# Single chunks beside the attention pairs of the last two layers, in place of groups

## The reference, cut to what matters

```python
h = rms_norm(x, norm_mix_pre)
proj = h @ w_in                      # dq, dk, dv, mq, mk, mv, c_q, c_kv, k_pe, g
oa = diff_attention(dq1, dq2, dk1, dk2, dv, lam, bias)   # 4 heads, softmax1 - lam * softmax2
oa = rms_norm(oa, diff_subln) * (1 - lam_init)
ob = moba_attention(mq, mk, mv, bias)                    # 4 heads, one block here: causal
oc = causal_attention(q_of(c_q), k_of(c_kv, k_pe), v_of(c_kv))   # "mla", 8 heads
br = [oa @ w_branch[0], ob @ w_branch[1], oc @ w_branch[2]]
mixed = sum(sigmoid(g[i]) * br[i]) @ w_out
x = x + rms_norm(mixed, norm_mix_post)
h = rms_norm(x, norm_mlp_pre)
x = x + rms_norm(square(relu(h @ w_up)) @ w_down, norm_mlp_post)
```

## Time and profile before

| | us |
|---|---|
| median of three runs | 3230.31 |
| lowest, highest | 3227.36, 3231.82 |
| the profiled run | 3227.58 |
| its span, from the first to the last instruction | 3225.8 |
| busy of the span: PE, DVE, ACT | 3094.3, 1801.9, 1152.2 |
| mean granted clock of PE | 0.974 |

### The profile page before, as it was taken

The page is one execution under the profiler, slowest core; times in us unless marked ns, Lnnn a source line. Parts: engine busy times, 40 slices in busy tenths (PEclk is TensorE's granted clock), DMA queues, the critical chain, the costliest instruction groups (busy, mean ns, idle before and its releaser), DMA issues. The chain is left out here.

```text
span 3225.8 us, 45812 instructions
## 1 busy us (share of the span) xinstructions
PE 3094.3 (96%) x18901; PEld 2696.4 (84%) x18901; DVE 1801.9 (56%) x3335; ACT 1152.2 (36%) x1943; POOL 62.2 (2%) x106
## 2 busy tenths in 40 slices
PE   7999999999989999999999898999999999999998
PEld 4788887888867888878888787999788999888998
DVE  1767665435447896643333444556656665656565
ACT  2322223223323222232222444444444444354443
POOL 1000000000000000000000100000001000001000
PEclk9899999999999999999999899999999999999999
DMA  8346442122124566532423323566335454435452
GB/s 272 109 133 183 138 156 89 42 83 92 59 66 135 167 213 183 180 101 72 117 76 109 91 81 84 166 179 196 98 100 183 147 190 133 131 92 167 135 183 92
DMA packets 501207, 421.28 MB, mean 131 GB/s; under 512 B 9946, under 2 KB 497674, under 8 KB 501000
## 3 DMA queue, kind: packets, MB, share of 16 engines
q1 hardware_dynamic: 497976, 412.33, 41.8%
q0 software_dynamic: 3024, 6.03, 0.8%
HBM read 417.20 MB, written 1.12 MB: 130 GB/s over the span
## 5 line engine op out<-in xcount | busy, mean ns | idle before, releaser
L1271 DVE TENSOR_TENSOR w_low<-raw,w_high 128x1024 fp32r<-128x1024 f32 (+2 forms) x720 | 761.4, 1099 | 367.0 <-ACT w_high L857 365.6
L857 ACT ACTIVATE w_high<-raw 128x1024 fp32r<-128x1024 f32 (+2 forms) x720 | 648.3, 950 | 689.9 <-PE gemm L1881 410.3
L1881 PE MATMUL gemm<-xh,w_high 128*128 128x512 f32 (+1 forms) x1792 | 676.6, 378 | 21.0 <-DVE xl L1307 21.0
L1881 PE MATMUL gemm<-xl,w_high 128*128 128x512 f32 (+1 forms) x1792 | 666.7, 372 | 0.0
L1881 PE MATMUL gemm<-xh,w_low 128*128 128x512 f32 (+1 forms) x1792 | 666.2, 372 | 0.0
L1881 PEld LDWEIGHTS gemm<-xh,w_high 128*128 128x128 f32 x1792 | 341.4, 191 | 92.1 <-issue 17.3
L1881 PEld LDWEIGHTS gemm<-xh,w_low 128*128 128x128 f32 x1792 | 341.7, 191 | 63.1
L1881 PEld LDWEIGHTS gemm<-xl,w_high 128*128 128x128 f32 x1792 | 342.2, 191 | 60.3 <-issue 0.7
L1881 PE MATMUL gemm<-yh,w_high 128*128 128x256 f32 x1216 | 351.3, 289 | 16.3 <-DVE yl L1332 7.1
L1881 PE MATMUL gemm<-yl,w_high 128*128 128x256 f32 x1216 | 346.3, 285 | 0.0
L1881 PE MATMUL gemm<-yh,w_low 128*128 128x256 f32 x1216 | 345.7, 284 | 0.0
(11 more groups left out here) (326 smaller groups left out, 4224.6 us busy)
## 6 DMA issues: line engine op xcount, KB each, us to landing
raw<-in_ffn_w_in SPq DMA_DIRECT2D x176, 512.0 KB, 5.2
raw<-in_w_mod SPq DMA_DIRECT2D x72, 1024.0 KB, 7.0
raw<-in_w_in SPq DMA_DIRECT2D x50, 1024.0 KB, 5.3
raw<-in_w_up SPq DMA_DIRECT2D x32, 1024.0 KB, 5.5
raw<-in_w_down SPq DMA_DIRECT2D x32, 1024.0 KB, 5.1
raw<-in_ffn_w_out SPq DMA_DIRECT2D x32, 768.0 KB, 4.7
raw<-in_ret_w_in SPq DMA_DIRECT2D x24, 1024.0 KB, 5.2
raw<-in_ffn_w_out SPq DMA_DIRECT2D x32, 640.0 KB, 4.3
```

The source lines that it names most:

```text
L857: act.activation(wh[i % SPL][:, a:b], raw[slot_of["w", i]][:, a:b], ACT.Copy).then_inc(w_high, 1)
L1271: dve.tensor_tensor(wl[slot][:, a:b], raw[slot][:, a:b], wh[i % SPL][:, a:b].bitcast(F32), ALU.subtract).then_inc(w_low, 1)
L1881: ins = pe.matmul(out, l_, r_, start=first and j == 0, stop=last and j == 2)
```

## The change

`alongside` gets a rule for each kind of attention: with x the step, diff has (x + 1) // 2 items done, moba min(4, 1 + (x + 1) // 2), mla x + (x + 1) // 2; nat keeps its own. All three engines pass by_chunk=True to the projections beside diff and mla, so that an item is a chunk: 8 beside diff, 24 beside mla. gate0 is stepped by chunks too; where one `next` stood, two stand. Its last four chunks run beside moba through `alongside`, on ACT and DVE with lag 1. On PE a small generator puts the wait for the scaled diff outputs (sub_t) behind moba's first scores, as before.

```diff
--- before.py
+++ after.py
@@ -669,11 +669,11 @@
 
 
             a = atts[name]
-            na, nb = 2 * len(a.pairs), 24 if a.nat else 4 if a.kind == "dif" else 12
             done = 0
-            for x in range(na + 1):
+            for x in range(2 * len(a.pairs) + 1):
                 next(steps)
-                upto = min(nb, x - x // 13) if a.nat else 1 + x * (nb - 2) // na
+                upto = {"nat": min(24, x - x // 13), "dif": (x + 1) // 2, "mob": min(4, 1 + (x + 1) // 2),
+                        "mla": x + (x + 1) // 2}[a.kind]
                 while done < upto - lag:
                     next(rest)
                     done += 1
@@ -1186,23 +1186,24 @@
                 run(gemm(f"diff_v{l}1"))
                 run(gemm(f"mla_ukv{l}"))
                 run(gemm(f"moba_q{l}"))
-                alongside(f"diff{l}", attention(f"diff{l}"), both(*(gemm(o) for o in with_diff(l))), 1)
-
-                gate = gemm(f"gate0{l}")
+                alongside(f"diff{l}", attention(f"diff{l}"), both(*(gemm(o, by_chunk=True) for o in with_diff(l))), 1)
+
+                gate = gemm(f"gate0{l}", by_chunk=True)
                 for hd in range(DH):
                     act.wait_ge(o_high, atts[f"diff{l}"].p0 + 2 * hd + 2)
                     act.activation(yt[:, hd, :], oraw[:, hd, :], ACT.Square).then_inc(sub_sq, 1)
+                next(gate)
                 next(gate)
                 act.wait_ge(sub_ms, l + 1)
                 act.activation(root8[:, :], aux[3][:, 0:8], ACT.Sqrt, bias=eps[:, 0:1],
                                scale=1.0 / P).then_inc(sub_root, 1)
                 next(gate)
+                next(gate)
                 for hd in range(DH):
                     act.wait_ge(sub_t, DH * l + hd + 1)
                     act.activation(ah[:, hd, :], oraw[:, hd, :], ACT.Copy, scale=1.0 - LAM_INIT[l]).then_inc(sub_high, 1)
-                run(attention(f"moba{l}"))
-                run(gate)
-                alongside(f"mla{l}", attention(f"mla{l}"), both(*(gemm(o) for o in with_mla(l))), 1)
+                alongside(f"moba{l}", attention(f"moba{l}"), gate, 1)
+                alongside(f"mla{l}", attention(f"mla{l}"), both(*(gemm(o, by_chunk=True) for o in with_mla(l))), 1)
                 for q in range(4):
                     run(gemm(f"gate2{l}{q}"))
                     run(gemm(f"branch2{l}{q}"))
@@ -2224,9 +2226,10 @@
                 pe.wait_ge(h_update, norms[f"c{l}"]["up0"])
                 pe.wait_ge(t5_in, 128)
                 wait_gemm_out(pe, f"diff_v{l}1")
-                alongside(f"diff{l}", attention(f"diff{l}"), both(*(gemm(o) for o in with_diff(l))))
-
-                gate = gemm(f"gate0{l}")
+                alongside(f"diff{l}", attention(f"diff{l}"), both(*(gemm(o, by_chunk=True) for o in with_diff(l))))
+
+                gate = gemm(f"gate0{l}", by_chunk=True)
+                next(gate)
                 next(gate)
                 for hd in range(DH):
                     pe.wait_ge(sub_sq, DH * l + hd + 1)
@@ -2245,19 +2249,19 @@
                         ins = pe.matmul(aux[2 + hd // 2][:, o:o + P],
                                         inv8[:, 2 * hd + j:2 * hd + j + 1].to_broadcast([P, P]), ident, start=True, stop=True)
                 ins.then_inc(sub_row, 1)
-                steps = attention(f"moba{l}")
                 wait_gemm_out(pe, f"moba_v{l}1")
-                next(steps)
-                next(gate)
-                pe.wait_ge(sub_t, DH * (l + 1))
-                for x in range(2 * len(atts[f"moba{l}"].pairs)):
-                    next(steps)
-                run(steps)
-                run(gate)
+
+                def behind_subln(steps):
+
+                    yield next(steps)
+                    pe.wait_ge(sub_t, DH * (l + 1))
+                    yield from steps
+
+                alongside(f"moba{l}", behind_subln(attention(f"moba{l}")), gate)
                 pe.wait_ge(roped, 2 * MH * (l + 1))
                 pe.wait_ge(sub_low, DH * (l + 1))
                 pe.wait_ge(o_low, atts[f"moba{l}"].p1)
-                alongside(f"mla{l}", attention(f"mla{l}"), both(*(gemm(o) for o in with_mla(l))))
+                alongside(f"mla{l}", attention(f"mla{l}"), both(*(gemm(o, by_chunk=True) for o in with_mla(l))))
                 for q in range(4):
                     run(gemm(f"gate2{l}{q}"))
                     pe.wait_ge(o_low, atts[f"mla{l}"].p1)
```

## The result

The changed kernel took 3209.42 us (median of 4 runs, 3207.02 to 3211.68), the kernel before beside it 3229.16 us (4 runs, 3227.36 to 3231.82). The ratio is 0.9938, with a 95% interval of 0.9921 to 0.9955: 19.7 us faster, forecast were 14.9. The same kernel measured a second time gave 0.9935 (0.9921 to 0.9948). The profiled run took 3210.51 us with a span of 3208.7 us, 17.1 us less than the span before.

The account below looks back on a forecast made before the run. PE, busy 96% of the span, was taken as the bound, so only its waits and clock falls could give time. 2 x (-3.0 + 0.8 - 4.5) - 1.5 = -14.9 us gave 3215.4 us from 3230.3, range 3207 to 3226.

Parts of the forecast that it names:

- likeliest case: Whole kernel: the forecast's own case around 3215.4 us, spanning 3211 to 3220 us, chance 0.57.
- the sign: Profile after, last two layers' attention stretches: idle PE time of 6 to 8 us each, length 146 to 147 us.
- Diff, -3.0 a layer: Diff pairs: waits of 5.5 us fall to 2.5, left only at scores(1) (1.7) and the last values (0.8).
- Sub-norm, 0: Between diff and moba: same four gate0 chunks, squares (1.3 us) covered by two chunks (5.8 us), nothing gained or lost.
- Moba, +0.8 a layer: Moba pairs: waits of 4.3 us instead of 3.5, copies queued behind tanh and split; bounds -2 and +2.
- Mla, -4.5 a layer: Mla pairs: all 4.5 us of waits go, covered by three chunks per pair; bounds -4.5 and -1.5.
- The clock, -1.5: PE's granted clock: one of two falls, after diff and at moba's end, goes, -1.5 us; bounds -3.0 and +1.5.
- The end of moba falls: Moba's end: 3 us of waits in some 5 us in both layers, so a clock fall was expected to remain.
- the second rival: Waits return behind ACT's and DVE's queues in mla and moba, clock falls in both layers: 3224 us, chance 0.2.
- More is won: Tanh does not hold up moba's copies and the clock does not fall: 3210 us, chance 0.15.
- The waits come back: Mla's DVE lag uncovered, moba pair 1 waits too, clock falls in both layers: 3224 us, chance 0.2.
- Slower by falls: Short steps alternating with chunks make the clock fall repeatedly, slower from 14 falls; one per diff and moba pair 3250 us; chance 0.04.

Follow-up runs that it names:

- The ends: Four kernels: changed kernel with chunks moved to the bare starts and ends of attention stages, dealt out differently each time; 3208.71, 3214.88, 3201.23 and 3194.15 us.
- the first two forms: Changed kernel, four branch chunks moved to moba's end, two gate0 chunks (then one) to diff, moba lag 2, mla's chunks respread; 3208.71, then 3214.88 us.
- the fourth: Changed kernel, moba lag 2, four branch chunks at moba's end, mla respread, diff's ends covered by one gate0 chunk, squares ahead of its split; 3194.15 us.
- lag 2: Changed kernel with ACT and DVE taking the gate chunks beside moba two chunks later instead of one; 3205.98 us, again 3207.87 us.
- moba alone: Kernel before with only moba's part: gate0 by single chunks, the last four beside moba, results one chunk later; 3230.17 us, ratio 1.0005.
- mla alone: Kernel before with only mla's part: branch0, gate1 and branch1 by chunks, results one chunk later; 3215.29 us, ratio 0.9957.
- diff alone: Kernel before with only diff's part: moba_k and moba_v by chunks, one beside each diff pair, results one chunk later; 3221.21 us, ratio 0.9977.
- moba undone: Changed kernel with moba and gate0 as in the kernel before (gate0 by groups, moba bare); 3207.55 us, ratio 0.9938.
- the ends' third form: Changed kernel, diff untouched, moba lag 2, four branch chunks at moba's end, mla's other 20 spread to keep the last split behind the last division; 3201.23 us.

## Why the prediction was right, point by point

The direction, the place and most of the sizes of the waits held. In the profiled runs the span fell by 17.1 us, forecast were 14.9. The median, 3209.4 us, is 6 us under the 3215.4 of the forecast and just under its likeliest case (3211 to 3220), inside the range only with room that was made for a rival. The waits of a stretch, 6.4 us, lie in the 6 to 8 that were named as the sign; its length, 144.9 us, lies under the 146 to 147. By the prediction's own terms:

- **Diff, -3.0 a layer.** The sum is right (2.48 us left, forecast 2.5), its parts aren't quite. scores(1) waits 1.48 instead of 1.7 and values(7) 0.55 instead of 0.8, each 0.2 less: I took PE as free at the start of the matmul that came next before the change, while its idle time begins only where the last pipelined matmul ends. The 0.45 at values(6) I had overlooked. The rule (x + 1) // 2 puts no chunk between any turn(p) and values(p): the chunk comes behind values. For pairs 0 to 5 the scores of pair p + 2 stand there; pairs 6 and 7 have nothing, and I saw only pair 7. In the timeline values(6) follows turn(6) directly, with the eighth chunk behind it. The two errors cancelled, so that the sum came out is luck.
- **Sub-norm, 0.** Right; no wait stands there. The ends show what that rests on: with one or two chunks fewer the first two forms lost 2 us there, and the fourth, with one fewer but the squares ahead of the split, lost nothing.
- **Moba, +0.8 a layer.** Right in kind, sized a little too high: 0.85, 1.13, 0.77, 1.14 for 1.1, 1.5, 0.8, 0.85, 3.9 us for 4.3, so +0.4. Alone it gave +1.9 us for both layers, within the noise. The tanh ahead of the copy is the cause of the first and of half of the second: with lag 2 they fell to nothing and to 0.56.
- **Mla, -4.5 a layer.** Right: no wait left; alone -4.5 a layer in waits. DVE didn't fall behind by so much that PE waited.
- **The waits together.** Forecast 13.4 us less, measured 13.50 + 13.63 - 2 x 6.37 = 14.4.
- **A term I left out: the empty pipeline.** The stretches got shorter by 16.3 us, the waits by 14.4. Stretch less waits was 139.4 us a layer with 16 waits and is 138.5 with 7. A wait costs on average some 0.1 us beside its idle time, which the profile books as busy; this is 1.9 us. The experiments put it in order: 139.4 with 17 waits (moba alone), 139.3 with 12 (mla alone), 138.7 with 10 (diff alone), 138.5 with 7 and with 6 (changed, moba undone), each with one clock fall. It isn't the same for each wait: diff's six fewer are worth 0.7 us and mla's four fewer 0.2. No idle time too short for the waits' list stands behind it; in before and in the changed kernel the listed waits are all of PE's idle time in the stretch.
- **The clock, -1.5: wrong.** Diff's fall did go, as argued, but that of layer 0 came back at the bare end of moba (2365), and that of layer 1 stands at scores(1) of diff (2788) instead of moba's end. Two falls before, two after: 0. "The end of moba falls" held for one layer, "in diff the short steps are parted" overlooked the 1.48 us at its own start, which is the longest wait of the stretch. So the term failed, and a fall in each layer is what the second rival had taken.
- **Outside the stretches** 0.8 us are gone. The falls there lie otherwise than before (the granted clock lost 1.9 us less in all); what moved them stays open.

Sum: -14.9 - 1.0 (waits) - 1.9 (pipeline) + 1.5 (clock) - 0.8 (outside) = -17.1 us. The medians differ by 19.7; the 2.6 us between are within the spread of the runs (4 to 5 us for each kernel). What was forecast too high in the clock was more than made up by what was forecast too low in the waits and left out in the pipeline; that the total is near rests in part on this.

**The rivals.** "More is won" gave 3210 us, and the median is 3209.4, but not by its mechanism: the tanh did hold up moba's copies, and the clock did fall. "The waits come back" did not happen in the changed kernel; it did in two of my own. "Slower by falls" did not happen: one clock fall stands in each stretch of the changed kernel, where 14 were needed in all. The Trainium skill, "TensorE: Matmul & The Clock Gate", section "A second HAM failure mode: psum-queue depth-cycling", describes such a swing for another kernel; no run here shows it beside single chunks.

## What to carry to other kernels

On an engine that is the bound, look for every consumer at what stands between it and its producer, and deal the fillers out to the bare places, the first and the last pairs above all: here the middle was covered throughout, and all seven waits that were left stood at the ends of stages or beside a tanh. Then walk the queues of the other engines for the same places, because a chunk brings its split and its tanh with it; chunks moved without that (two forms here) only moved the wait, and with it (two others) they were worth 8 and 15 us. How much of the gain is the finer cut into chunks and how much the other places was not tested apart: no run keeps the groups and deals them out otherwise. Where PE's waits fall below 1 us each, look at the granted clock before you expect the time to follow.

## What the hardware showed that I had not expected

- **A short wait costs more than its idle time.** Within a chunk the matmuls of 256 columns start 0.12 us apart and last 0.28 us each in the profile; when PE runs into a wait, the last one's remaining 0.16 us are not overlapped and count as busy. The runs show about 0.1 us for a wait on average; that this remainder is its cause is argued, not shown. The Trainium skill, "TensorE: Matmul & The Clock Gate", section "Single matmul latency", gives (398 + N) / 2.4 ns at the full clock for a single bf16 matmul, 0.27 us for 256 columns. The profile has 0.28 for these, but it models the ends of matmuls, so it does not measure this.
- **The clock falls in a fixed size.** Each fall in the stretches of before and of the changed kernel loses 1.7 us of granted clock (0.57 over 4.0 us), of which 1.5 to 1.6 were found in the time, with single idle times of no more than 1.6 us ahead of it. In the changed kernel's second profile they came back at moba's end and at the start of diff within a microsecond, and so did nearly all falls outside the stretches. In the two profiles of lag 2 they did not: one of the four stretches had none. The granted clock lost 76 to 92 us in each whole span.
- **Fewer waits can come with another fall.** 4.95 us of waits came with two falls in three stretches of four, and with none in the fourth, 6.4 us and 2.7 us (the ends' third form) with one. With 0.9 us there was none in either stretch. I can't say from these runs what sets it.
